# Gate and embedding weights as one block of ten k tiles in two slots of five

## What is computed

```python
x = layer_norm(ALPHA * x + 0.5 * swiglu(x, ffn1_w_in, ffn1_w_out))
z = x @ w_in                                  # then a pooling mixer and an RWKV-7 mixer
x = layer_norm(ALPHA * x + concat(pool, rwkv) @ w_out)
h = ALPHA * x + 0.5 * swiglu(x, ffn2_w_in, ffn2_w_out)
gate = sigmoid(h @ ple_gate_w + ple_gate_b)   # 1024 x 1024
h = h + gate * (p @ ple_w)                    # 256 x 1024
x = layer_norm(h)
```

## Time and profile before

| | us |
|---|---|
| median of 3 runs | 3031.05 (3028.4 to 3035.96) |
| the profiled execution | 3029.19 |
| its span, first to last instruction | 3027.2 |
| TensorE busy | 2735.7 (90%) |
| GpSimd busy | 1445.2 (48%) |
| VectorE busy | 1092.2 (36%) |
| ScalarE busy | 696.9 (23%) |
| mean granted TensorE clock | 0.955 of full speed |

### The profile page before, as it was taken

How to read it: one execution, slowest core, us unless ns; L and a number is a source line. 1 busy time by engine, 2 the same in 40 slices (tenths; PEclk the granted TensorE clock), 3 DMA queues, 4 the chain that set the end, 5 groups by cost and what they waited for, 6 DMA issues and landing times.

```text
span 3027.2 us, 68787 instructions
## 1 busy us (share of the span) xinstructions
PE 2735.7 (90%) x27640; PEld 2623.4 (87%) x27640; DVE 1092.2 (36%) x1448; ACT 696.9 (23%) x1193; POOL 1445.2 (48%) x932
## 2 busy tenths in 40 slices
PE   8999989888887899999799999898888888999995
PEld 8999979776776799999699999797777777999994
DVE  3222047545553422211432210575545434222124
ACT  3221021233421322200232210212343203221013
POOL 5555645422213455555555555454222145555553
PEclk9999999889997999999999999898999989999997
DMA  4232322100001132332222322120000012223321
GB/s 147 88 90 82 89 60 85 36 3 4 3 19 43 56 90 83 97 86 77 85 73 87 90 85 85 60 84 22 4 3 4 17 57 63 90 85 93 90 73 57
DMA packets 64112, 192.66 MB, mean 64 GB/s; under 512 B 11712, under 2 KB 14016, under 8 KB 63936
## 3 DMA queue, kind: packets, MB, share of 16 engines
q1 hardware_dynamic: 59904, 185.95, 20.5%
q10 hardware_dynamic: 4032, 4.08, 0.4%
HBM read 186.88 MB, written 3.12 MB: 63 GB/s over the span
## 4 chain that ended last, share of the span: by engine, by line
PE 73%; issue 14%; POOL 6%; DVE 4%; ACT 3%; DVEq 0%; ACTq 0%; DMA 0%; POOLq 0%; SPq 0%
PE ps L519 64%; PE ps L575 4%; PE ps L534 2%; POOL w_lo L464 1%; DVE xl L1192 1%; PE ps L679 1%; POOL w_hi L462 1%; DVE y L1188 1%; DVE rs L1177 0%; POOL nt L391 0%; POOL tA L397 0%; POOL Lb L423 0%; POOL nt L389 0%; PE ps L694 0%; ACT xh L887 0%
## 5 line engine op out<-in xcount | busy, mean ns | idle before, releaser
L519 PE MATMUL ps<-xh,w_hi 128*128 128x272 f32 x4032 | 848.7, 292 | 104.3 <-POOL w_lo L464 49.0
L464 POOL TENSOR_TENSOR w_lo<-w_raw,w_hi 128x1024 fp32r<-128x1024 f32 (+3 forms) x380 | 854.8, 2249 | 31.7
L519 PE MATMUL ps<-xh,w_lo 128*128 128x272 f32 x4032 | 838.7, 290 | 0.0
L519 PE MATMUL ps<-xl,w_hi 128*128 128x272 f32 x4032 | 838.4, 290 | 0.0
L462 POOL TENSOR_SCALAR w_hi<-w_raw 128x1024 fp32r<-128x1024 f32 (+3 forms) x380 | 374.0, 984 | 865.7 <-PE ps L519 856.4
L519 PEld LDWEIGHTS ps<-xh,w_hi 128*128 128x128 f32 x4032 | 639.2, 190 | 118.4 <-DVE xl L1192 54.9
L519 PEld LDWEIGHTS ps<-xl,w_hi 128*128 128x128 f32 x4032 | 640.8, 191 | 0.0
L519 PEld LDWEIGHTS ps<-xh,w_lo 128*128 128x128 f32 x4032 | 636.3, 190 | 0.0
L1144 DVE TENSOR_TENSOR hf<-sg,ps 128x544 f32<-128x544 f32 x88 | 63.5, 722 | 708.3 <-PE ps L519 708.3
L519 PE MATMUL ps<-hh,w_hi 128*128 128x272 f32 x1472 | 305.5, 289 | 0.0
L519 PE MATMUL ps<-hl,w_hi 128*128 128x272 f32 x1472 | 303.6, 287 | 0.0
(11 more groups left out here) (242 smaller groups left out, 3202.8 us busy)
## 6 DMA issues: line engine op xcount, KB each, us to landing
w_raw<-in_w1i SPq DMA_DIRECT2D x88, 512.0 KB, 3.5
w_raw<-in_w2i SPq DMA_DIRECT2D x88, 512.0 KB, 3.5
w_raw<-in_wz SPq DMA_DIRECT2D x44, 512.0 KB, 3.5
w_raw<-in_w1o SPq DMA_DIRECT2D x32, 448.0 KB, 3.4
w_raw<-in_w2o SPq DMA_DIRECT2D x32, 448.0 KB, 3.3
w_raw<-in_w1o SPq DMA_DIRECT2D x16, 512.0 KB, 3.5
w_raw<-in_wo SPq DMA_DIRECT2D x16, 512.0 KB, 3.6
w_raw<-in_w2o SPq DMA_DIRECT2D x16, 512.0 KB, 3.5
```

The costliest lines, as they stand in the source:

```text
L464: pool.tensor_tensor(w_lo[k][:, 0:nk, :], w_raw[k][:, 0:nk, :], w_hi[k][:, 0:nk, :].bitcast(F32), ALU.subtract).then_inc(w_split, 1)
L519: mm = pe.matmul(ps[:, 2 * pair + h, 0:HT], w[:, j, :], x[:, k0 + j, h * HT:(h + 1) * HT], start=(part == 0 and j == 0 and q == 0), stop=( ...
```

## The change

- The gate weights and the embedding weights of one output tile lie in memory as one block of ten k tiles (eight gate, two embedding), and are read as two slots of five. The second slot holds gate tiles 5 to 7 and both embedding tiles. An output tile has two slots in place of three, the stage 16 per layer in place of 24. The number and the order of the matmuls stay.
- The end of the gate product now falls inside a slot, so the eighth gate tile's last matmul signals a semaphore of its own, `gate_mm`, and ScalarE waits for that.
- TensorE's wait for the embedding banks moves inside the second slot, ahead of the ninth k tile.
- ScalarE's loop of four rounds is written out as eight sigmoids in a row.
- The three products of a k tile stand in a helper, `three`, that `dense` uses too (its matmuls are on line 490).

```diff
-          ("f2i", FT, [8, 8]), ("f2o", 4, [8, 7, 7, 8, 7, 7]), ("gp", 4, [4, 4, 2, 4, 4, 2])]
+          ("f2i", FT, [8, 8]), ("f2o", 4, [8, 7, 7, 8, 7, 7]), ("gp", 4, [5, 5, 5, 5])]
...
-                                tile = bass.ds(l * 8 + m * 2 + i // 3, 1)
-                                src = wp[tile] if i % 3 == 2 else wg[tile, :, i % 3 * 4:i % 3 * 4 + 4, :]
+                                src = wgp[bass.ds(l * 8 + m * 2 + i // 2, 1), :, 5 * (i % 2):5 * (i % 2) + 5, :]
...
+            def gates(l, hi, lo, ready, base):
+                def body(m, first):
+                    for i in range(4):
+                        k, part = i % 2, i % 2
+                        n = l * SLOTS + SLOT0["gp"] + m * 4 + i
+                        if part == 0:
+                            pe.wait_ge(tile_out[0], out_count(l, "gp", m * 2 + i // 2) - 1)
+                        pe.wait_ge(w_split, n + 3)
+                        for j in range(5):
+                            c = 5 * part + j
+                            pair, x_hi, x_lo, kx = (0, hi, lo, c) if c < 8 else (1, hh, hl, c - 8)
+                            if c == 8:
+                                pe.wait_ge(tile_out[1], out_count(l, "gp", m * 2 + i // 2) - 1)
+                                if first and i == 1:
+                                    pe.wait_ge(pl_ready, l * 2 + 2)
+                            if first and i < 2 and c < 8:
+                                pe.wait_ge(ready, base + c + 1)
+                            mm = three(pair, k, j, x_hi, x_lo, kx, c in (0, 8), c in (7, 9))
+                            if c == 7:
+                                mm.then_inc(gate_mm, 1)
+                        mm.then_inc(slot_used, 1)
+                body(0, True)
+                with pe.Fori(1, 4) as m:
+                    body(m, False)
...
-                with act.Fori(0, 4) as m:
+                for m in range(4):
                     for k in range(2):
-                        act.wait_ge(slot_used, used_count(l, "gp", 6 * m + (3 * k + 1)))
+                        act.wait_ge(gate_mm, l * 8 + 2 * m + (k + 1))
                         act.wait_ge(tile_out[1], out_count(l, "gp", 2 * m + k) - 1)
                         act.activation(halves(sg[:, :]), pair_bank(0), ACT.Sigmoid, bias=col(l, 2 * m + (k + COL["gate_b"]))).then_inc(tile_out[0], 1)
...
-                        dve.wait_ge(slot_used, used_count(l, "gp", 6 * m + (3 * k + 2)))
+                        dve.wait_ge(slot_used, used_count(l, "gp", 4 * m + (2 * k + 1)))
...
-        "wg": flat_slots(slots(a["ple_gate_w"])), "wp": flat_slots(slots(a["ple_w"])),
+        "wgp": flat_slots(np.concatenate([slots(a["ple_gate_w"]), slots(a["ple_w"])], axis=3)),
```

More of the change, by code:

```diff
@@ L71, with build @@
 UNITS_OF = [range(0, 4), range(4, 9)]
-def build(nc, xT, pT, w1i, w1o, wz, wo, w2i, w2o, wg, wp, params, consts, poolw, lora_w, g2_w,
+def build(nc, xT, pT, w1i, w1o, wz, wo, w2i, w2o, wgp, params, consts, poolw, lora_w, g2_w,
           pool_hist, shift_hist, wkv_hist, y_out, pool_out, shift_out, wkv_out):
@@ L207, in build @@
         w_loaded = [sem(f"w_loaded{i}") for i in range(2)]
-        w_hi_done, w_split, slot_used = sem("w_hi_done"), sem("w_split"), sem("slot_used")
+        w_hi_done, w_split, slot_used, gate_mm = sem("w_hi_done"), sem("w_split"), sem("slot_used"), sem("gate_mm")
         tile_out = [sem(f"tile_out{i}") for i in range(2)]
@@ L486, in constants_there, with three @@
                 pe.wait_ge(loaded, 16 * NLOAD)
+            def three(pair, k, j, x_hi, x_lo, kx, start, stop):
+                for q, (w, x) in enumerate(((w_hi[k], x_hi), (w_hi[k], x_lo), (w_lo[k], x_hi))):
+                    for h in range(2):
+                        mm = pe.matmul(ps[:, 2 * pair + h, 0:HT], w[:, j, :], x[:, kx, h * HT:(h + 1) * HT],
+                                       start=(start and q == 0), stop=(stop and q == 2))
+                return mm
+            def gates(l, hi, lo, ready, base):
[22 more added lines that the diff above has]
+                    body(m, False)
             def dense(l, name, hi, lo, ready, base, start=0, end=None):
@@ L497, in body @@
                         k, pair, part, tile = i % 2, i // per, i % per, m
-                        if name == "gp":
-                            pair, part, tile = i % 3 // 2, i % 3 % 2, m * 2 + i // 3
                         n = l * SLOTS + SLOT0[name] + m * B + i
@@ L503, in body @@
                             pe.wait_ge(tile_out[pair], out_count(l, name, tile) - 1)
-                        if name == "gp" and i == 2 and first:
-                            pe.wait_ge(pl_ready, l * 2 + 2)
                         pe.wait_ge(w_split, n + 3)
-                        embedding = name == "gp" and pair == 1
-                        x_hi, x_lo = (hh, hl) if embedding else (hi, lo)
-                        k0 = (0, 4)[part] if name == "gp" else (0, 8, 15)[part]
-                        last_part = part == (1 if name == "gp" else per - 1) or embedding
+                        k0 = (0, 8, 15)[part]
                         for j in range(nk):
@@ L516, in body @@
                                 pe.wait_ge(ready, base + k0 + j + 1)
-                            for q, (w, x) in enumerate(((w_hi[k], x_hi), (w_hi[k], x_lo), (w_lo[k], x_hi))):
-                                for h in range(2):
-                                    mm = pe.matmul(ps[:, 2 * pair + h, 0:HT], w[:, j, :], x[:, k0 + j, h * HT:(h + 1) * HT],
-                                                   start=(part == 0 and j == 0 and q == 0),
-                                                   stop=(last_part and j == nk - 1 and q == 2))
+                            mm = three(pair, k, j, hi, lo, k0 + j, part == 0 and j == 0, part == per - 1 and j == nk - 1)
                         mm.then_inc(slot_used, 1)
@@ L843, in _ @@
                 dense(l, "f2o", hh, hl, hl_ready, l * (2 * FT) + FT)
-                dense(l, "gp", xh, xl, xl_ready, l * 40 + 32)
+                gates(l, xh, xl, xl_ready, l * 40 + 32)
                 norm(l * 3 + 2)
```

## The result

The changed kernel has a median of 3013.21 us (3007.63 to 3018.61), the kernel before 3031.05 (3028.4 to 3035.96), five executions of each side by side. The ratio is 0.9939 with a 95% interval of 0.9922 to 0.9956, that is 18.5 us less on 3031.05. The forecast was 3018.1 us with a range from 3013 to 3026. Faster was right. The profiled execution took 3010.22 us with a span of 3008.4, against 3029.19 and 3027.2.

What follows compares the result with a forecast made beforehand. TensorE, busy 90% of the span, bounds the kernel, with removable pauses in gp. Per layer 3 x 1.19 (table loads) + 3 x 0.96 (GpSimd's split) = 6.45 us, 12.9 in all: median 3018.1 us, range 3013 to 3026.

Steps and rivals of the forecast that it cites:

- the two formulas: gp stage, from an output tile's start: ScalarE's chain 7.41 us, 8.71 with a table load; GpSimd's split chain 8.46.
- Part one, the table loads: gp: three of four table loads per layer go, sigmoid hides with 0.09 us to spare; gain 3.6 us per layer.
- Part two, slots of five: gp: GpSimd's chain of 2.85 us fits in 3.76, so its wait goes at three tiles; gain 2.9 us per layer.
- VectorE beside GpSimd: gp: split beside VectorE's product and sums; a 0.37 us stretch leaves 0.5 of 0.9 us to spare; nothing charged.
- Rival two: gp: VectorE's sums hold up GpSimd's split, TensorE stops 0.56 us at 14 of 16 tiles; 3025.9 us, chance 0.08.
- The DMAs: gp weight loads: 320 KB lands in 2.9 us where 5.15 us are available; nothing charged.
- The signal, the moved wait, the start of the stage: gp: gate semaphore bounded at zero to one TensorE restart, embedding-bank wait already satisfied, start keeps 2 us to spare.
- The drain behind a table load: ScalarE: a skill page's drain of about 1380 ns would mean 2.8 us less gain; forecast followed the trace, without drain.
- rival one: gp: sigmoid just late, TensorE stops 0.1 to 0.2 us per tile, 1.2 to 2.4 us lost; about 3020, chance 0.12.
- (three): Rival, gp on ScalarE: a table load's time still spent in each pair, 7.1 us stay; 3025.2 us, chance 0.03.
- (four): Rival, gp: a slot's DMA becomes the bound, 35 us slower, 3066 us; chance 0.04 including any other unseen loss.
- The sum: Both gp gains together: 6.45 us per layer, 12.9 us for two layers.

Runs made afterwards that it cites:

- six copies: Changed kernel plus six one-column ScalarE copies ahead of each gp sigmoid; one profiled execution, span 3011.1 us, output tile starts 7.76 us apart in the mean.
- six and four: Changed kernel with gp slots of six and four k tiles in place of five and five; one execution 3007.59 us, starts 7.75 to 7.77 us apart.

## Why the prediction missed its range

**What bounds the kernel, and the two formulas: right.** The second profile of the kernel before repeats 8.71 and 8.48 us in both layers. With changed inputs the formulas said 8.48 (unrolled loop), 7.83 (six copies) and 7.85 (six and four), and the runs gave 8.47, 7.76 and 7.76.

**Part one, the table loads: right in sum, the margin mis-sized.** Two loads are left, the others follow without. The sigmoid is hidden with 0.18 us to spare, not 0.09. In the written-out rounds the two queue instructions of ScalarE's wait have medians of 35 and 46 ns, where the kernel before has 77 and 103, so the sigmoid and the load start some 0.1 us earlier. The new semaphore has no part in it: the unrolled loop alone, which still waits for `slot_used`, also has 35 and 46 ns, and the slots of five alone, which wait for `gate_mm` in the loop, have 68 and 103. That gave the first output tile 0.10 us per layer that the sum did not have; the restart, which the sum didn't count at the tile after the last stop, took it back. That the 3 x 1.19 belong to this part is true only with part two there: alone it is worth 3 x 0.23.

**Part two, slots of five: right.** 0.73 and 1.56 us were taken for the split and measured. 0.9 us to spare was worked out, 1.05 is there. Alone it is worth its 2.9 us per layer by the starts.

**VectorE beside GpSimd: the cost of nothing was right, the reason only in part.** Rival two asked whether GpSimd waits. The stretch went wholly to VectorE (2.05 us for a sum), which has 7.5 us per output tile. By the Trainium skill, page "SBUF — State Buffer", section "SBUF: two separate sides", the engine that starts first gets the shared ports for its whole instruction, and the other waits. The sum that starts 0.10 us after `w_lo` and ends 0.58 us after `w_lo`'s end agrees with it to some 0.15 us, since alone it takes 0.73. The prediction found that the 1.64 us of `w_lo` at 2952.06 agreed with the rule only in part. It had looked at `ysum` alone, and the sum `y` had started 0.24 us ahead of that `w_lo`:

```profile
2951.82 0.73 DVE L1456 TENSOR_TENSOR y<-y,hf 128x544 f32 x1
```

It ended 0.49 us into the `w_lo`, which took 0.37 longer than usual. So who starts first decides here, and after the change that is GpSimd, by only 0.10 us. Had VectorE been first, the split might have lost up to one sum, 0.73 us (an estimate from this row), of the 1.05 to spare. No run made it so.

**The DMAs: right,** 2.9 us to landing as forecast, no wait for one in gp.

**The signal, the moved wait, the start of the stage: right,** no stop at the ninth k tile, and from the first gp matmul (2905.72) to the second output tile's start it is 8.49 us.

**The drain behind a table load: not there.** The Trainium skill, page "ScalarE: Activation LUTs", section "What ACT_TABLE_LOAD costs", would have a drain of about 1380 ns behind the load. The sigmoid at 2913.37 follows the load's end (2912.08 + 1.28) within 0.01 us, and so does the one-column sigmoid at 1421.05 (1419.76 + 1.28). The measurement decides.

**The rivals.** None came about: no stop for the sigmoid behind the one that was forecast (one), none for a split (two), two loads and no more (three), and the DMAs in time (four). A stop of rival one's kind costs about what it said: with six copies, which put the sigmoid 0.5 us later, the starts come 0.25 us further apart than with one to three. Rivals one and two stayed away by 0.18 us and by an order of 0.10 us.

**The sum: right by every trace.** 6.46 us per layer in the gp stage where 6.45 was forecast, 12.3 us in the spans without the recurrence, and 0.9957 as a ratio (3018.1 to 3031.05) beside 0.9939, 0.9949 and 0.9962 measured. That it agrees to the hundredth is luck in part: 0.10 us for the earlier table load at the first output tile and 0.10 for the restart behind it were both left out and cancel.

**The step that failed is the last one, from the sum to a median and its range:** "3013 (the forecast less 5 for the scatter of a median)". The mechanism was right, and the term that was too small is these 5 us. Two things were wrong in it.

- *The base was taken as the kernel's time.* The forecast stands on 3031.05 us, the median shown. The same kernel's medians beside later runs were 3026.09, 3027.05 and 3026.39 us. So by these the base alone was some 4.5 us high, nearly all of the 5 us that the range allowed. From 3026.5 the same sum gives 3013.6, and the changed kernel's three medians are 3013.21, 3011.80 and 3014.68.
- *The scatter was charged for one median alone.* A comparison has it in both of its medians. The prediction had three executions of one kernel for it (7.6 us from the lowest to the highest). In the later runs single executions of the kernel before went from 3015.03 to 3036.62, one layer's recurrence from 535.48 to 548.93 in the five profiles above, and each comparison with the changed kernel is uncertain by some 5 us to either side. The trace of before showed where it arises, since the mean clock was 0.91 in one layer's recurrence and 0.93 in the other's with the same instructions, a difference of 6.4 us; the prediction looked at the clock of the gp stage only.

That the miss is 0.4 us and no more, and that there is one, is chance: with the second or the third ratio the time would be 3015.6 or 3019.5 us on the same base, inside the range.

**What stays open.** The three ratios have a mean of 0.9950, or 15 us, where the spans without the recurrence give 12.3 and the gp stage 12.9. Each comparison is uncertain by 5 us, so this needs no further cause, but one of 2 us outside gp is not excluded. Whether the high base of the first comparison was chance among five executions, or belongs to the chip on which they ran, the runs don't tell.

## What to carry to other kernels

When two waits of nearly the same length take turns on the critical path, work out both chains for every turn. One may lie under the other, as GpSimd's did here under the table load; removing the upper one alone then gives only the difference (1.6 us here), while removing the lower one pays in full where it stands alone (5.8 us). The table load inside the loop body came back in every round here (8 loads, 2 when written out); written-out rounds, and a one-column activation placed earlier, took it off the path. Before a forecast for a gain of 0.5%, look in the trace for stages whose time differs between identical layers, and put that scatter on both ends of the range and on the base. Compare the stage that was changed by itself: 61.20 against 67.66 us said in one trace what the medians could not.

## What the runs showed of the hardware that I had not expected

- TensorE's granted clock in a stage with pauses differs between executions of the same program: the same 6819 matmuls took 535.48 us at a mean of 0.94 and 548.93 us at 0.90, within one execution.
- A GpSimd `w_lo` of 640 columns that started 0.10 us ahead of VectorE's sum was not stretched (1.56 to 1.57 us), while the sum took 2.05 in place of 0.73 us. Behind a VectorE instruction GpSimd is stretched: in the changed kernel a `w_hi` at 2909.80, while VectorE makes `hl`, took 1.09 in place of 0.73 us.
- One-column copies in a row on ScalarE take 0.19 to 0.20 us each in the trace but start 0.09 us apart.
- f1o and f2o take 132.5 us each in eight profiles and 131.3 or 131.9 in the six of kernels with one small tile more. The output tiles of gp, 7.53 us apart in the changed kernel, are 7.51 apart there.
- The same kind of semaphore wait on ScalarE cost 0.1 us less in the written-out rounds (35 and 46 ns in its queue) than in the loop (77 and 103 ns), whichever semaphore it was for.
